# Each token is closed in its second expert block; the last pass over the residual goes

## The reference, cut to what matters

```python
x = x + jnp.einsum('bse,ed->bsd', mix, w_out)
x = x + _hier_moe(_rmsnorm(x, g_ffn), w_router_group, w_router_expert, w_exp_gate, w_exp_up, w_exp_down)
...
y = (silu(xb @ w_g[e]) * (xb @ w_u[e])) @ w_d[e]      # each token: sum of two of these, each times its gate
...
return _rmsnorm(x, g_final)
```

## Time and profile before

| what | us |
|---|---|
| median of 3 runs | 1694.93 (1692.10 to 1695.05) |
| the profiled execution, its own time | 1697.46 |
| its span (first to last instruction) | 1696.0 |
| add of block 2 to add of block 26, 24 blocks | 449.3, so 18.7 a block |
| last add into `x_mid` starts | 1655.4 |

### The profile page before, as it was taken

How to read it: one execution, slowest core, us unless ns; L and a number is a source line. 1 busy time by engine, 2 the same in 40 slices (tenths; PEclk the granted TensorE clock), 3 DMA queues, 4 the chain that set the end, 5 groups by cost and what they waited for, 6 DMA issues and landing times.

```text
span 1696.0 us, 21534 instructions
## 1 busy us (share of the span) xinstructions
PE 1493.7 (88%) x7474; PEld 1245.8 (73%) x7474; DVE 1096.3 (65%) x1617; ACT 877.2 (52%) x1144; POOL 227.1 (13%) x226
## 2 busy tenths in 40 slices
PE   6999999999956699996799974999999999999970
PEld 5888788888856578884588863787877777778860
DVE  5655655444335467673355554988888888888864
ACT  6433433332324454452343352877777777777744
POOL 0000111101110000000012222132222111121210
PEclk9999999999987799997799986999999999999995
DMA  7122412122113100001643453999999999999958
GB/s 245 58 92 91 153 57 69 61 67 67 44 49 127 62 32 13 19 13 53 245 169 114 145 191 113 343 388 372 388 384 378 376 374 379 372 379 387 390 146 306
DMA packets 80068, 327.05 MB, mean 193 GB/s; under 512 B 13747, under 2 KB 23987, under 8 KB 55299
## 3 DMA queue, kind: packets, MB, share of 16 engines
q1 hardware_dynamic: 63282, 278.82, 43.8%
q0 software_dynamic: 16720, 47.40, 9.4%
HBM read 281.71 MB, written 53.90 MB: 198 GB/s over the span
## 4 chain that ended last, share of the span: by engine, by line
DMA 20%; PE 12%; DVE 10%; issue 5%; ACT 4%; SPq 0%; ACTq 0%; DVEq 0%; POOLq 0%; POOL 0%
DMA plain<-in_w_down 18%; DVE split L1537 8%; PE acc L93 4%; PE acc L94 3%; PE acc L95 3%; PE acc L1723 1%; ACT split L2148 1%; ACT plain L2181 1%; ACT split L1531 1%; DMA plain<-s_w_fold 0%; PE acc L1716 0%; ACT plain L1761 0%; DMA s_table<-plain 0%; DMA s_x_mid<-plain 0%; DMA plain<-in_w_out 0%
## 5 line engine op out<-in xcount | busy, mean ns | idle before, releaser
L1537 DVE TENSOR_TENSOR split<-plain,split 128x2048 fp32r<-128x2048 f32 x192 | 428.3, 2284 | 4.9 <-ACT split L1531 4.9
L93 PE MATMUL acc<-split 128*128 128x512 f32 x960 | 387.8, 404 | 34.1 <-DVE split L1786 23.6
L1531 ACT CAST split<-plain 128x2048 fp32r<-128x2048 f32 x192 | 363.5, 1916 | 82.9 <-DMA plain<-in_w_up 50.6
L95 PE MATMUL acc<-split 128*128 128x512 f32 x960 | 380.2, 396 | 0.0
L94 PE MATMUL acc<-split 128*128 128x512 f32 x960 | 380.2, 396 | 0.0
L93 PEld LDWEIGHTS acc<-split 128*128 128x128 f32 x960 | 184.2, 192 | 75.4 <-issue 27.8
L95 PEld LDWEIGHTS acc<-split 128*128 128x128 f32 x960 | 183.9, 192 | 39.9
L94 PEld LDWEIGHTS acc<-split 128*128 128x128 f32 x960 | 184.1, 192 | 36.1
L93 PE MATMUL a_p<-a_w_hi,a_xT_hi 128*128 128x512 f32 (+1 forms) x480 | 194.7, 406 | 4.1 <-DVE a_w_lo L679 4.1
L95 PE MATMUL a_p<-a_w_hi,a_xT_lo 128*128 128x512 f32 (+1 forms) x480 | 186.9, 389 | 0.0
L94 PE MATMUL a_p<-a_w_lo,a_xT_hi 128*128 128x512 f32 (+1 forms) x480 | 186.3, 388 | 0.0
(11 more groups left out here) (281 smaller groups left out, 2380.7 us busy)
## 6 DMA issues: line engine op xcount, KB each, us to landing
plain<-in_w_gate SPq DMA_DIRECT2D x64, 1024.0 KB, 10.2
plain<-in_w_up SPq DMA_DIRECT2D x64, 1024.0 KB, 12.3
plain<-in_w_down SPq DMA_DIRECT2D x64, 1024.0 KB, 10.8
a_x_sb<-in_x SPq DMA_DIRECT2D x24, 512.0 KB, 3.9
s_mid<-a_kv SPq DMA_DIRECT2D x12, 512.0 KB, 2.9
a_kv<-s_mid SPq DMA_DIRECT2D x12, 512.0 KB, 3.6
plain<-s_mixT SPq DMA_DIRECT2D x12, 512.0 KB, 5.9
plain<-in_x SPq DMA_DIRECT2D x12, 512.0 KB, 3.7
```

The source lines that it names most:

```text
L93: pe.matmul(out, st_hi, mv_hi, start=first, stop=False)
L95: return pe.matmul(out, st_lo, mv_hi, start=False, stop=last)
L1531: eng.copy(self.w_hi[:, j // 2, cols], self.raw[:, j // 2, cols]).then_inc(self.s_whi[j], 1)
L1537: eng.tensor_tensor(self.w_lo[:, j // 2, cols], self.raw[:, j // 2, cols], self.w_hi[:, j // 2, cols].bitcast(F32), ALU.subtract).then_inc ...
```

## The change

- **The table.** An entry has four words in place of two: row, gate, the row at which to add, the row at which to close. For the expert of a token that comes second (`closes`), the add row is out of bounds, and so the DMA skips it; for the first, the close row is. `queue` works these out with six more small DVE instructions.
- **Adds.** `add_rows` adds only the first contribution of each token.
- **Closing, in the loop.** For block n, POOL gathers the partial rows from `x_mid` into `xp[half]` (`gather_sums`), adds `y_sb` (a POOL tensor_tensor of 128x1024, gives `s_z`), ACT squares and sums (`square`), DVE finds the reciprocal root in 12 small instructions by Newton steps (`invert`), ACT scales the row (`scale`), POOL multiplies by `g_final` (again 128x1024), and an indirect DMA stores the rows to `out` (`keep_rows`).
- **Places.** Iteration n of POOL starts the gather of sums of block n-2 and closes block n-3. Step n of ACT and of DVE squares, inverts and scales block n-4.
- **take_y** is done by ACT alone, both halves in one instruction; DVE's part goes. PE gives out three quarters of the down product ahead of turning the hidden rows.
- **The end.** The load of `x_mid`, the 12 squares, roots and scales and the 12 stores go. The last blocks are closed behind the loop, blocks 29, 30 and 31 by DVE.

```diff
@@ POOL, close and gather
+            def gather_sums(half, index, buf):
+
+                settle_waits(pool, s_tick)
+                pool.indirect_dma_start(out=buf[:], out_offset=None, in_=x_rows,
+                                        in_offset=bass.IndirectOffsetOnAxis(ap=index, axis=0),
+                                        bounds_check=ROWS - 1, oob_is_err=False).then_inc(s_xp[half], 16)
...
+            def close_rows(n, r, half, index):
+
+                pool.wait_ge(s_xp[half], 16 * (r + 1))
+                settle_waits(pool, s_tick)
+                nc.gpsimd.tensor_tensor(xp[half][:], xp[half][:], y_sb[half][:], ALU.add).then_inc(s_z, 1)
+                pool.wait_ge(s_scaled, n + 1)
+                settle_waits(pool, s_tick)
+                nc.gpsimd.tensor_tensor(xp[half][:], xp[half][:], g_row[:], ALU.mult).then_inc(s_out, 1)
+                pool.wait_ge(s_out, n + 1)
+                settle_waits(pool, s_tick)
+                keep_rows(half, index, xp[half])
@@ POOL, iteration n
                 if n >= 2:
+                    pool.wait_ge(ex.s_pairs, 1)
+                    if n >= 3:
+                        pool.wait_ge(s_store[1 - half], 16 * ((n - 3) // 2 + 1))
+                    if n >= 4:
+                        pool.wait_ge(s_kept[half], 16 * ((n - 4) // 2 + 1))
+                    gather_sums(half, lists[:, n - 2, 3:4], xp[half])
+                if n == 3:
+                    pool.wait_ge(s_const, 16)
+                if n >= 3:
+                    close_rows(n - 3, (n - 3) // 2, 1 - half, lists[:, n - 3, 3:4])
+                if n >= 2:
                     pool.wait_ge(s_store[half], 16 * (n // 2))
                 if n:
-                    add_rows(n - 1, 1 - half, lists[:, n - 1, 0:1])
+                    add_rows(n - 1, 1 - half, lists[:, n - 1, 2:3])
@@ ACT
-                nc.scalar.activation(y_sb[half][:, 0:512], py[:, 0:512], ACT.Copy,
+                if not (isinstance(r, int) and r == 0):
+                    act.wait_ge(s_z, n - 1)
+                nc.scalar.activation(y_sb[half][:], py[:], ACT.Copy,
                                      scale=gate[half][:, 0:1]).then_inc(s_ya, 1)
+
+            def square(n, buf):
+                act.wait_ge(s_z, n + 1)
+                act.wait_ge(s_newton, 11 * n)
+                nc.scalar.activation(junk[:], buf[:], ACT.Square, accum_out=ssq[:]).then_inc(s_sq, 1)
+
+            def scale(n, buf):
+                act.wait_ge(s_rstd, n + 1)
+                nc.scalar.activation(buf[:], buf[:], ACT.Copy, scale=rstd[:, 0:1]).then_inc(s_scaled, 1)
@@ ACT, step n
                 if again:
                     split(0, n)
+                if not (isinstance(r, int) and r < 2):
+                    square(n - 4, xp[half])
                 rows_hi(n)
                 if again:
                     split(1, n)
                     split(2, n)
+                    if not (isinstance(r, int) and r < 2):
+                        scale(n - 4, xp[half])
                     split(3, n)
@@ DVE, step n
                     split(1, n)
+                    if not (isinstance(r, int) and r < 2):
+                        invert(n - 4)
                     split(2, n)
                     split(3, n)
...
-                    take_y(n - 2, r - 1, half)
@@ POOL, after the loop
+            gather_sums(0, closing[0][:, 3:4], xp[0])
+            pool.wait_ge(s_out, 2 * prev + 2)
+            settle_waits(pool, s_tick)
+            keep_rows(1, closing[1][:, 3:4], xp[1])
+            pool.wait_ge(s_store[0], 16 * prev + 32)
+            pool.wait_ge(s_wlo[0], 2 * prev + 4)
+            gather_sums(1, code[1][:, 3:4], xp_last)
```

More of the change, by code:

```diff
@@ L41 @@
 EPS = 1e-6
+MAGIC = float(0x5F3759DF)
 M_KT, M_V, M_CT = 0, 512, 1024
@@ L1510, in __init__ @@
         self.ident = sb([P, P])
[L1511 to L1514, removed]
+        self.g_row = sb([P, D])
+        self.lists = sb([P, NE, 4], I32)
+        self.late, self.code, self.closing = ([sb([P, 4], I32) for _ in range(2)] for _ in range(3))
         self.gate = [sb([P, 1]) for _ in range(2)]
-        self.ssq, self.root, self.rstd = sb([P, TILES]), sb([P, TILES]), sb([P, TILES])
+        self.ssq, self.mean, self.root, self.part, self.rstd = (sb([P, 1]) for _ in range(5))
+        self.bits = sb([P, 1], I32)
         self.blocks = sb([1, 2, NBLK], I32)
@@ L1928, in phase_experts @@
         s_silu, s_h, s_ht, s_hhi, s_hlo = (sem(n) for n in ("silu", "h", "ht", "hhi", "hlo"))
[L1929 to L1932, removed]
+        s_ya = sem("ya")
+        s_xp, s_kept = ([sem(f"{n}{i}") for i in range(2)] for n in ("xp", "kept"))
+        s_z, s_sq, s_newton, s_rstd, s_scaled, s_out, s_noted = (
+            sem(n) for n in ("z", "sq", "newton", "rstd", "scaled", "out", "noted"))
         span = raw_span
@@ L1939, in each_block @@
         def each_block(eng, body):
-            for half in range(2):
-                body(0, half)
+            for r in range(3):
+                for half in range(2):
+                    body(r, half)
             eng.wait_ge(ex.s_pairs, 1)
-            with eng.Fori(1, pair_count(eng)) as r:
+            with eng.Fori(3, pair_count(eng)) as r:
                 for half in range(2):
@@ L1963, in step @@
                 n = 2 * r + half
[L1964 to L1967, removed]
+                if not (isinstance(r, int) and n == 0):
                     load(n, expert(n), range(4))
+                if not (isinstance(r, int) and n <= 1):
                     load(n - 1, expert(n - 1), (4, 5))
             each_block(sp, step)
[L1972 to L1984, removed]
+            prev = sp.value_load(n_pairs[0:1, 1:2], min_val=NE // 2 - 2, max_val=(NE + MORE + 1) // 2)
+            load(2 * prev + 3, expert(2 * prev + 3), (4, 5))
         @block.gpsimd
@@ L1990, in _ @@
             by_place = table.rearrange("(r x) a -> r (x a)", x=NE)
+            out_rows = out.rearrange("t p n -> (t p) n")
             def gather_rows(half, index):
@@ L2169, in _ @@
             each_block(act, step)
-            last = act.value_load(n_pairs[0:1, 1:2], min_val=0, max_val=(NE + MORE + 1) // 2)
-            take_y(2 * last, last, 0)
-            late(2 * last + 1, False)
-            take_y(2 * last + 1, last, 1)
-            act.wait_ge(s_eps, 1)
-            for t in range(TILES):
-                act.wait_ge(s_xmid[t // 2], 16)
-                act.wait_ge(s_rstd, t)
-                one = slice(t, t + 1)
-                nc.scalar.activation(junk, x_sum[t], ACT.Square, accum_out=ssq[:, one]).then_inc(s_sq, 1)
-                act.wait_ge(s_sq, t + 1)
-                nc.scalar.activation(root[:, one], ssq[:, one], ACT.Sqrt, bias=eps[:],
-                                     scale=1.0 / D).then_inc(s_root, 1)
+            prev = act.value_load(n_pairs[0:1, 1:2], min_val=NE // 2 - 2, max_val=(NE + MORE + 1) // 2)
+            take_y(2 * prev + 2, prev + 1, 0)
+            late(2 * prev + 3, False)
+            square(2 * prev, xp[0])
+            scale(2 * prev, xp[0])
+            square(2 * prev + 1, xp[1])
+            take_y(2 * prev + 3, prev + 1, 1)
+            square(2 * prev + 2, xp[0])
+            square(2 * prev + 3, xp_last)
         @block.vector
```

154 lines of the change are left out of this document (98 added, 56 removed).

## The result

The changed kernel takes **1968.8 us** in the median of 4 runs (1967.2 to 1972.2), the kernel before 1695.0 beside it (4 runs, 1692.1 to 1698.7): a ratio of 1.16, 95% interval 1.157 to 1.163. The profiled execution has a span of 1970.7 us. TensorE's granted clock is 0.905 of full speed in the mean, 0.935 before.

The account below looks back on a forecast made before the run. The prediction took the weights' DMA, 18.7 us a block, to bound the kernel before, and a ring of waits the changed one. Its terms summed to +285 on 1697.5, 1982, given as 1980 us; forecast 1940 to 2020, range 1820 to 2030.

Parts of the forecast that it names:

- closed ring of waits: Expert stage: waits through POOL, ACT and DVE, once a block, take 28.4 us where the weights take 18.7.
- 1. 24 blocks: Steps 5 to 28 of the expert stage: 28.4 less 18.7, 9.7 us each, +233 us.
- 2. step 4: First step with a square, no multiply and store ahead of the add yet: +6 us.
- 3. two table reads: POOL iterations 28 and 29: list reads between copy and gather, 6 us each plus 9.7 a block, +32 us.
- 4. the end: From the add of block 28 to the span's end: about 101 us where it was 89, +12 us.
- 5. the mix: Six more small DVE instructions in queue, exposed in the last tile, with a larger list load: +2 us.
- the bare ring: Per block, the waits through POOL, ACT and DVE without any contention: 21.5 to 21.7 us.
- taken as hidden: Store of block n-4 lands before the gather of sums, having 9.6 us; bounded at +3 us a block.
- first rival: Only sums contend at the port, or nothing does: 21.7 to 22.7 us a block, 1805 to 1829 us; chance 0.22.
- what should show it: Profile signs: adds 26 to 30 us apart, DMA share about 0.65, ACT idle 6 to 9 us, issues 2 to 3 us.

Follow-up runs that it names:

- No port waits: Changed kernel, DVE's splits from block 1 on subtract PSUM columns, so only one input is in SBUF (wrong values): 1883.2 us, block 24.7 us.
- own buffer: Changed kernel, POOL's multiply writes to a buffer of its own, from which the rows are stored: 1972.7 us, block 27.4 us.
- Neither: Changed kernel, POOL's sum and multiply cut to one column and DVE's splits given one SBUF input: 1812.3 us, block 22.0 us in the mean.
- The order of the end: Changed kernel, POOL's last two iterations put sum, table read and gather of h rows ahead of multiply and store: 1953.8 us.
- No sums on POOL: Changed kernel, POOL's sum and multiply by g cut to one column, waits and issues kept: 1875.1 us, block 24.5 us.

## Why the prediction was right, point by point

**The mechanism** was right: a closed ring of waits, not a full engine. That the total came so near is in part luck. Forecast 1980, measured 1968.8; the ratio of slowdown was 1.168 in the forecast and is 1.16. But the terms of the sum were off by -24, +5, -6, +19 and -4 us, and cancel to -10. In the profiled execution:

| Term | forecast | measured | from |
|---|---|---|---|
| 1. 24 blocks | +233 | +208.5 | (657.8 - 449.3) |
| 2. step 4 | +6 | +11 | adds of blocks 1 and 2, 28.8 apart, 17.75 before |
| 3. two table reads | +32 | +26.2 | adds 26 to 28: 62.3, before 36.1 |
| 4. the end | +12 | +30.8 | add of 28 to the end of the span: 119.9, before 89.1 |
| 5. the mix, to the add of block 1 | +2 | -1.9 | this add's start (1101.8, before 1103.7); the first gather +1.6 |

- **Term 1 was 1 us a block too large** (27.4, not 28.4). The sum on POOL takes 2.38 us, not 2.6: I had doubled a 1.30 of half the size and noted 2.4 as the other end. It also began directly behind the issue, where I had left 0.3, and the multiply had ended 0.4 us earlier than I laid out. The parts are as forecast: 5.95 us of port waits came off POOL's rows (No port waits), and 27.4 less these is 21.5, the bare ring of the prediction. With port waits and landing both gone POOL's stretch from multiply to sum takes 11.4 us, where I had 11.5.
- **The Trainium skill**, "SBUF — State Buffer", Who interferes with whom, was weighed in the prediction, and the trace went against it for the issues: without DVE's second SBUF input the store and the two gathers are 0.8 to 1.9 us shorter. (The add, which met no split, takes 1.58 either way.) The Trainium skill also has, on the same page under "Summary: rules for kernel authors", that the second one to issue is fully blocked until the first is through. With this the trace agrees: split 2 ends at 1453.8, and the multiply, 2.40 us long when undisturbed, ends 2.3 us behind it, at 1456.0, 0.7 late; split 3, 2.28 us long when undisturbed, ends 2.2 us behind that, 1.3 late. I had put split 3 at over 2 us late; that was too much.
- **The landing of the store, "taken as hidden"**, was right for the changed kernel (own buffer: no change), but for a reason that I had not seen. I argued that the queues would have room. It is hidden since POOL's issues are themselves late. Take the port waits away and it stands open with 3.56 us.
- **So the first rival was mis-sized.** "The ring without waits of the issues" had 21.7 to 22.7 us and 1805 to 1829. With the waits gone it is 24.7 us and 1883 (No port waits). And 21.7 us, when at last reached with the landing taken out, is held there by a second ring of ACT and DVE (scale, split 3, y, splits 4 and 5 and the hidden rows on ACT; then the hidden rows, four splits, the product, rows_lo and the root on DVE) that I had not added up; that it has nearly the length of the first is chance. The 19.0 us that I expected of Neither missed this ring.
- **Terms 2 and 3.** A table read in the ring cost 3.8 us a block, not 6. Why step 4 took 5 us more than counted stays open.
- **Term 4 was the step that failed.** I followed POOL's chain to the last store and counted 101 us; it was 119.9. (The parts that the prediction lists, 79 and 25, would even be 104.) I gave the rows of block 32 no wait on PE's side, and had y of block 30 only 20 us behind the root of block 27. POOL issues the gather of these rows only behind the store, its landing, the closing list, the gather of sums and the table read. The gather of sums, which I had landed 3 us behind its issue, took 7.8 us from the end of its issue, and the rows come when PE has stood for 19.9 us. With POOL reordered (The order of the end) this end takes 96.6 us.
- **Of what should show it**, adds were 27.4 apart (26 to 30 forecast), ACT's wait ahead of the square 8.5 us in the mean (6 to 9), issues 1.8 to 3.0 where they met a split (2 to 3). DMA share was 0.79, not 0.65; by bytes, 272 of 380 GB/s, it is 0.72, so a byte took about a tenth more of the queues' time.

## What to carry to other kernels

When a change puts a step of one engine between two steps of another, write down the order of each engine and walk round the loop until you are back at the same instruction of the next block: if the walk is longer than the block, the walk is the new block, however idle the engines are. Then look for the second longest walk and for waits that the first one hides, since they are what a mend will meet: here 5.95 us of port waits hid 3.6 us of a store's landing, and behind both stood a ring of two other engines. Work that takes the place of a tail of 35 us may cost 1.2 us in each of 28 blocks, and less than that if it has a tail of its own: with the ring broken the blocks cost 14 us more, and the end was 5 us shorter, not 35.

## What I had not expected of the hardware

- A column copy or an indirect issue on POOL waits for the split that DVE has in hand when both of the split's inputs are in SBUF, up to 1.9 us each, and is undisturbed (0.75, 1.00 to 1.08) as soon as one input is in PSUM. The split itself takes the same 2.28 us either way.
- The indirect store of 128 rows holds its buffer for longer than the add, the copy and the gather behind it take when nothing delays them: 8.4 us in the median from issue to landing (No sums on POOL), 3.5 us past the moment when the next gather was ready.
- Two loads of ACT's tables a block, 1.28 us each, were cheaper than 11 small DVE instructions of about 0.2 us where DVE was full: 1755 to 1714 us.
